# Re-timing the first transfers of a two-block transformer kernel and writing out the last turn of its branch loop

## The reference

```python
h = rmsnorm(x, g_pre_mix[l])
proj = h @ w_in[l]
(cb, cc, cv, q, k, v, qm, ga, gb, gc) = jnp.split(proj, IN_OFFSETS, axis=-1)
y_a = (cb * causal_dwconv(cc * cv, conv_mix_w[l])) @ w_conv_out[l]
...
y_b = jnp.transpose(o, (0, 2, 1, 3)).reshape(b_, s_, ATT_W) @ w_attn_out[l]
y_c = memory_attention(qm, rmsnorm(mem, g_mem[l]), w_mem_kv[l]) @ w_mem_out[l]
merged = (jax.nn.sigmoid(ga + bg[0]) * y_a + jax.nn.sigmoid(gb + bg[1]) * y_b
          + jax.nn.sigmoid(gc + bg[2]) * y_c)
x = x + rmsnorm(merged @ w_out[l], g_post_mix[l])
```

## Time and profile before

| | before |
|---|---|
| time, median of 3 runs | 1634.99 us |
| lowest and highest run | 1633.8 and 1635.36 us |
| time of the profiled execution | 1635.36 us |
| its span in the trace | 1633.6 us |
| PE busy | 1567.8 us, 96% of the span |
| DVE busy | 901.2 us, 55% |
| ACT busy | 627.0 us, 38% |

### The profile page before, as it was taken

One profiled execution on the slowest core, in us unless ns is written; L12 is line 12 of the kernel. 1 busy time (PEld: TensorE's weight loads), 2 busy tenths in 40 slices (PEclk: granted clock), 3 DMA queues, 4 the chain that ended last, 5 costly groups with the idle time before them and its releaser, 6 DMA issues.

```text
span 1633.6 us, 20708 instructions
## 1 busy us (share of the span) xinstructions
PE 1567.8 (96%) x7842; PEld 1311.6 (80%) x7842; DVE 901.2 (55%) x1441; ACT 627.0 (38%) x862; POOL 11.8 (1%) x16
## 2 busy tenths in 40 slices
PE   5999999999999899999999889998989999999999
PEld 5888787888877688888888767998878788888887
DVE  4443465544553877776532857978965444434322
ACT  5451434332233444444332535564463323232211
POOL 0000000000000000000000000000000000000000
PEclk9999999999999899999999999999999999999999
DMA  8312221222222122222322312202002222222222
GB/s 291 125 77 103 75 75 52 103 85 95 103 83 97 52 103 92 90 101 103 129 103 103 118 52 77 78 26 74 31 27 89 92 103 101 81 101 103 103 103 77
DMA packets 25705, 150.18 MB, mean 92 GB/s; under 512 B 2563, under 2 KB 4995, under 8 KB 9260
## 3 DMA queue, kind: packets, MB, share of 16 engines
q1 hardware_dynamic: 25644, 149.35, 26.1%
HBM read 147.21 MB, written 2.13 MB: 91 GB/s over the span
## 4 chain that ended last, share of the span: by engine, by line
PE 83%; DVE 9%; ACT 4%; issue 2%; SPq 1%; DMA 1%; DVEq 0%; ACTq 0%
PE bank L1676 25%; PE bank L1678 25%; PE bank L1677 25%; ACT w_hi L569 2%; PE bank L1790 2%; PE bank L2074 1%; PE bank L1770 1%; DVE w_lo L1033 1%; PE bank L2011 1%; DVE sel L1452 1%; DVE st L1451 1%; DMA raw<-weights 1%; PE bank L1779 1%; DVE w_lo L1041 1%; DVE mx L1163 0%
## 5 line engine op out<-in xcount | busy, mean ns | idle before, releaser
L1676 PE MATMUL bank<-h_hi,w_hi 128*128 128x512 f32 (+1 forms) x1200 | 475.7, 396 | 12.6 <-DVE h_lo L1106 9.9
L1033 DVE TENSOR_TENSOR w_lo<-raw,w_hi 128x2048 fp32r<-128x2048 f32 x118 | 270.3, 2291 | 369.3 <-ACT w_hi L569 368.9
L1678 PE MATMUL bank<-h_hi,w_lo 128*128 128x512 f32 (+1 forms) x1200 | 469.2, 391 | 0.0
L1677 PE MATMUL bank<-h_lo,w_hi 128*128 128x512 f32 (+1 forms) x1200 | 468.9, 391 | 0.0
L569 ACT ACTIVATE w_hi<-raw 128x2048 fp32r<-128x2048 f32 x128 | 244.5, 1910 | 345.7 <-PE bank L1678 342.5
L1676 PEld LDWEIGHTS bank<-h_hi,w_hi 128*128 128x128 f32 (+1 forms) x1200 | 225.5, 188 | 67.6 <-DVE h_lo L1106 9.4
L1678 PEld LDWEIGHTS bank<-h_hi,w_lo 128*128 128x128 f32 (+1 forms) x1200 | 225.5, 188 | 48.7
L1677 PEld LDWEIGHTS bank<-h_lo,w_hi 128*128 128x128 f32 (+1 forms) x1200 | 225.7, 188 | 47.3 <-issue 0.9
L1676 PE MATMUL bank<-a_hi,w_hi 128*128 128x512 f32 x352 | 136.9, 389 | 0.0
L1677 PE MATMUL bank<-a_lo,w_hi 128*128 128x512 f32 x352 | 136.9, 389 | 0.0
L1678 PE MATMUL bank<-a_hi,w_lo 128*128 128x512 f32 x352 | 136.9, 389 | 0.0
(11 more groups left out here) (283 smaller groups left out, 1913.1 us busy)
## 6 DMA issues: line engine op xcount, KB each, us to landing
raw<-weights SPq DMA_DIRECT2D x128, 1024.0 KB, 4.8
toep<-bias_scratch SPq DMA_DIRECT2D x8, 448.0 KB, 4.4
x<-xT SPq DMA_DIRECT2D x1, 2048.0 KB, 18.0
x_tok<-x_tok SPq DMA_DIRECT2D x1, 2048.0 KB, 15.9
outT<-x SPq DMA_DIRECT2D x8, 256.0 KB, 4.2
memT<-memT SPq DMA_DIRECT2D x2, 512.0 KB, 5.9
...
```

The lines of the kernel that those rows point to most:

```text
L1033: nc.vector.tensor_tensor(w_lo[m % 2][:, :], raw[m % 2][:, :], w_hi[m % 2][:, :].bitcast(F32), ALU.subtract).then_inc(lo_ready, 1)
L1676: nc.tensor.matmul(o, lh, rh, start=first, stop=False)
L1677: nc.tensor.matmul(o, lh, rl, start=False, stop=False)
L1678: return nc.tensor.matmul(o, ll, rh, start=False, stop=last)
```

## The change

It has two parts. At the start, `memT` and load 0 come in three pieces each (a quarter, a quarter, a half: `PIECES`), rounded and split piece by piece; `x` comes in two halves; load 2 is issued ahead of `x`, load 3 between the two halves and load 4 behind them, ahead of `x_tok`; `ident`, `onehot` and `rel_bias` come ahead of all of these; ACT and DVE round, split and scale in an order that follows this. In the branch loop the last of the three turns is written out as straight code on PE, ACT and DVE; in it ACT rounds the first four tiles of `merged` before it rounds the first load of `w_out`, and DVE makes the eight low parts between the last four merges instead of behind them.

```diff
@@ -463,26 +466,38 @@
                                  bass.AP(src.tensor, (2 * pair + j) * 1024, [[1, P], [1, 896]])
                                  ).then_inc(toep_in[pair % 2], 16)
 
-            def mem_half(c):
+            def mem_piece(c):
+                piece = slice(PIECES[c], PIECES[c + 1])
+                sp.dma_start(memT[:, piece, :], A["memT"].rearrange("(k p) t -> p k t", p=P)[:, piece, :]
+                             ).then_inc(mem_in[c], 16)
+
+            def raw_piece(c):
+                piece = slice(PIECES[c] * COLS, PIECES[c + 1] * COLS)
+                sp.dma_start(raw[0][:, piece], A["weights"][0, :, piece]).then_inc(raw_piece_in[c], 16)
+
+            def x_half(c):
                 half = slice(c * KT // 2, (c + 1) * KT // 2)
-                sp.dma_start(memT[:, half, :], A["memT"].rearrange("(k p) t -> p k t", p=P)[:, half, :]
-                             ).then_inc(mem_in[c], 16)
+                sp.dma_start(x[:, half, :], A["xT"].rearrange("(k p) t -> p k t", p=P)[:, half, :]).then_inc(x_in[c], 16)
 
             sp.dma_start(vec[:, :], A["vec"]).then_inc(vec_in, 16)
-            mem_half(0)
-            sp.dma_start(raw[0][:, 0:SLOT // 2], A["weights"][0, :, 0:SLOT // 2]).then_inc(raw_half, 16)
-            mem_half(1)
-            sp.dma_start(raw[0][:, SLOT // 2:SLOT], A["weights"][0, :, SLOT // 2:SLOT]).then_inc(raw_full[0], 16)
+            for c in range(3):
+                mem_piece(c)
+                raw_piece(c)
             load(1)
             sp.dma_start(mem_tok[:, :, :], A["mem_tok"].rearrange("(t p) d -> p t d", p=P)).then_inc(mem_tok_in, 16)
-            sp.dma_start(x[:, :, :], A["xT"].rearrange("(k p) t -> p k t", p=P)).then_inc(x_in, 16)
             sp.dma_start(ident[:, :], A["ident"]).then_inc(const_in, 16)
             sp.dma_start(onehot[0:NB + 1, :], A["onehot"]).then_inc(onehot_in, 16)
             sp.dma_start(relb[0:NB, :], A["rel_bias"]).then_inc(onehot_in, 16)
             sp.wait_ge(lo_ready, 1)
             load(2)
+            x_half(0)
+            sp.wait_ge(lo_ready, 2)
+            load(3)
+            x_half(1)
+            sp.wait_ge(lo_ready, 3)
+            load(4)
             sp.dma_start(x_tok[:, :, :], A["x_tok"].rearrange("(t p) d -> p t d", p=P)).then_inc(x_tok_in, 16)
-            stream(3, FIRST["v"] + 2)
+            stream(5, FIRST["v"] + 2)
 
             sp.wait_ge(bank_free[slot["bias", 1].bank], turn(("bias", 1)) + 1)
             sp.dma_start(A["bias_scratch"], bias_row[0:HEADS, :]).then_inc(bias_saved, 16)
@@ -655,18 +670,15 @@
             act.wait_ge(set_up, 1)
             nc.scalar.activation(st[:, 4, 15:16], ones[:, 0:1], ACT.Sqrt)
             act.wait_ge(vec_in, 16)
-            act.wait_ge(mem_in[0], 16)
-            for j in range(KT):
-                if j == KT // 2:
-                    act.wait_ge(mem_in[1], 16)
-                raised(mn_hi[:, j, :], memT[:, j, :], "g_mem", j)
-                if j == 1:
-                    act.wait_ge(raw_half, 16)
-                    nc.scalar.activation(w_hi[0][:, 0:SLOT // 2], raw[0][:, 0:SLOT // 2], ACT.Copy).then_inc(hi_half, 1)
-                if j == KT // 2:
-                    act.wait_ge(raw_full[0], 16)
-                    nc.scalar.activation(w_hi[0][:, SLOT // 2:SLOT], raw[0][:, SLOT // 2:SLOT], ACT.Copy
-                                         ).then_inc(hi_ready, 1)
+            for c in range(3):
+                act.wait_ge(mem_in[c], 16)
+                for j in range(PIECES[c], PIECES[c + 1]):
+                    raised(mn_hi[:, j, :], memT[:, j, :], "g_mem", j)
+                    if j == PIECES[c]:
+                        cut = slice(PIECES[c] * COLS, PIECES[c + 1] * COLS)
+                        act.wait_ge(raw_piece_in[c], 16)
+                        nc.scalar.activation(w_hi[0][:, cut], raw[0][:, cut], ACT.Copy
+                                             ).then_inc(hi_ready if c == 2 else hi_piece, 1)
 
             def token_squares(src, count, first):
 
@@ -678,18 +690,19 @@
             round_w(1)
             act.wait_ge(mem_tok_in, 16)
             token_squares(mem_tok, MT, 8)
-            act.wait_ge(x_in, 16)
+            root(MT, mean_ready, 1)
+            round_w(2)
             for j in range(KT):
+                if j % 4 == 0:
+                    act.wait_ge(x_in[j // 4], 16)
                 raised(h_hi[:, j, :], x[:, j, :], "g_pre_mix", j)
-                if j == 1:
-                    root(MT, mean_ready, 1)
-                    round_w(2)
-                if j == 5:
+                if j == 3:
+                    round_w(3)
+                if j == 4:
                     keep_rms("mem", rms_mem, M)
-                    round_w(3)
+            round_w(4)
             act.wait_ge(x_tok_in, 16)
             token_squares(x_tok, TT, 10)
-            round_w(4)
             act.wait_ge(rms_col, 1)
             for m in range(2):
                 for t in (2 * m, 2 * m + 1):
@@ -732,7 +745,13 @@
                 wait_own(("cb", t))
                 nc.scalar.activation(br_hi[:, t, :], cy[:, t, :], ACT.Copy).then_inc(rounded, 1)
 
-            with act.Fori(0, 3) as i:
+            def merged_hi(j):
+
+                act.wait_ge(merge_add, 4 + 16 + j + 1)
+                nc.scalar.activation(br_hi[:, j, :], merged[:, j, :], ACT.Copy).then_inc(rounded, 1)
+
+            def gates(i, last=False):
+
                 for half in range(2):
                     for m in range(3):
                         round_w(FIRST["branch"] + 3 * half + m + 1, i, 6)
@@ -743,10 +762,15 @@
                             nc.scalar.activation(gate[:, t, :], gate[:, t, :], ACT.Sigmoid,
                                                  bias=vec[:, bass.ds(8 * i + (VEC["b_gate"] + 4 * half + t), 1)]
                                                  ).then_inc(gated, 1)
-
-            for j in range(KT):
-                act.wait_ge(merge_add, 4 + 16 + j + 1)
-                nc.scalar.activation(br_hi[:, j, :], merged[:, j, :], ACT.Copy).then_inc(rounded, 1)
+                        if last and half and m == 1:
+                            for j in range(4):
+                                merged_hi(j)
+
+            with act.Fori(0, 2) as i:
+                gates(i)
+            gates(2, last=True)
+            for j in range(4, KT):
+                merged_hi(j)
             for m in range(4):
                 round_w(FIRST["w_out"] + m + 1)
                 for j in (2 * m, 2 * m + 1):
@@ -1204,26 +1228,29 @@
             dve.wait_ge(vec_in, 16)
             for j in range(KT):
                 low_gained(mn_lo[:, j, :], memT[:, j, :], "g_mem", mn_hi[:, j, :], j)
-                if j in (1, KT // 2):
-                    part_ = int(j > 1)
-                    cut = slice(part_ * SLOT // 2, (part_ + 1) * SLOT // 2)
-                    dve.wait_ge(hi_ready if part_ else hi_half, 1)
+                if j in PIECES:
+                    c = PIECES.index(j)
+                    cut = slice(PIECES[c] * COLS, PIECES[c + 1] * COLS)
+                    if c == 2:
+                        dve.wait_ge(hi_ready, 1)
+                    else:
+                        dve.wait_ge(hi_piece, c + 1)
                     nc.vector.tensor_tensor(w_lo[0][:, cut], raw[0][:, cut], w_hi[0][:, cut].bitcast(F32), ALU.subtract
-                                            ).then_inc(lo_ready if part_ else lo_half, 1)
+                                            ).then_inc(lo_ready if c == 2 else lo_piece, 1)
             split_w(1)
             dve.wait_ge(const_in, 16)
             token_norm(M, 8, 8)
+            split_w(2)
             for j in range(KT):
                 low_gained(h_lo[:, j, :], x[:, j, :], "g_pre_mix", h_hi[:, j, :], j)
-                if j == 1:
-                    split_w(2)
-                if j == 5:
+                if j == 3:
                     split_w(3)
-                    dve.wait_ge(bank_free[6], turn(("spread", "mem")) + 1)
-                    for t in (2, 3, 0, 1):
+                if j in (4, 6):
+                    for t in (2, 3) if j == 4 else (0, 1):
+                        dve.wait_ge(bank_free[6], turn(("spread", "mem")) + 1)
                         ready(("mem_k", t))
-                        frees(("mem_k", t), nc.vector.tensor_tensor(mk[:, t, :], B(("mem_k", t))[:, 0:M], rms_mem[:, :],
-                                                                    ALU.mult))
+                        frees(("mem_k", t), nc.vector.tensor_tensor(mk[:, t, :], B(("mem_k", t))[:, 0:M],
+                                                                    rms_mem[:, :], ALU.mult))
             split_w(4)
             token_norm(S, 10, 0)
             split_w(5)
@@ -1310,9 +1337,15 @@
                         dve.wait_ge(merge_add, 4 + 4 * half + t + 8 * i)
                         nc.vector.tensor_tensor(merged[:, 4 * half + t, :], merged[:, 4 * half + t, :],
```

(17 more changed lines are left out.)

17 lines of the change are left out of this document (11 added, 6 removed).

## The result

| | before | changed |
|---|---|---|
| time, median of 4 runs each on one chip | 1635.1 us | 1624.65 us |
| lowest and highest run | 1633.8 and 1635.36 us | 1623.29 and 1626.25 us |
| the profiled execution | 1635.36 us | 1623.29 us |

The ratio is 0.9934, with a 95% interval from 0.9922 to 0.9945: 10.5 us faster in the medians, 12.1 us between the two profiled executions. The forecast was 1622.9 us, with a range from 1620.3 to 1626.8.

A forecast was written before the change was run, and what follows sets the result against it. PE was taken as the bound, busy 1567.8 of 1633.6 us, so only its idle and low-clock stretches pay. 1635.36 - 11.7 (start) - 0.8 (join) = 1622.9 us, range 1620.3 to 1626.8.

The forecast's parts named there:

- The order of the transfers: Start: moving loads ahead of `x` and `x_tok` removes PE's waits; `qm` starts at 36.1, not 47.81, 11.7 us.
- The join: Last branch turn into first `w_out` tile: the 2.47 wait goes, split starts 2.2 later, gain 0.8; bounds +0.9 and -1.7.
- Load 2 ahead of `x`: Start: load 2 lands at 19.1, split by 23.4, before PE's 24.0; the 5.30 wait goes and PE stays at 2.4 GHz.
- Load 3 and `mk`: Start: load 3 lands at 24.3, `mem_k` banks free by 29.9, PE wants them at 30.3; 2.17 wait goes, 0.4 spare.
- A wait at load 3 for `mk`: Listed sign that the prediction is wrong: PE waiting at load 3 for `mk` or for the split.
- The pieces: Start: quarters of load 0 start PE near 7.5, but later landings stay the same; worth only 0.2 to 0.3 us.
- The rival of the longer low clock: Start: PE, fed in scattered bits, stays at 1.2 GHz, load 1 up to 4.7 us longer; 1625.5 to 1627.6, chance 0.12.
- `x_tok`: Start: issued behind load 4, lands at 34.7; load 5 split at 45.0, PE wants it at 48.0; hidden, 3 us spare.
- `ident`: Start: table ahead of `x` comes near 17, so the norm's root is out by 19.2, no longer waiting until 22.56.
- only as a bound: First `w_out` tile: -1.7 us, half of a 3.4 us stretch at clock 0.50 that isn't there, and no wait gap.
- Writing out the turn as such: Last branch turn: same PE matmuls, loop register instructions fall away; costed at nothing, hidden by matmuls without a gap.
- The sum: Whole kernel: profiled 1635.36 less 11.7 at the start and 0.8 at the join gives 1622.9 us.

The follow-up runs named there:

- run 1: Kernel before with only `memT` and load 0 in a quarter, a quarter and a half: 1635.14 us, ratio 1.0005.
- run 2: Changed kernel with `memT` and load 0 in two halves and the old branch loop, leaving the new order alone: 1623.87 us, ratio 0.9935.
- run 3: Kernel before with only the last branch turn written out and the low parts dealt in: 1635.31 us, ratio 1.0001.
- run 5: Like run 2, but only load 2 moved ahead; loads 3 and 4 behind all of `x` and `x_tok`: 1632.48 us, ratio 0.9982.
- Run 9: Run 7 with the first two `mk` tiles right behind load 3's split on DVE, ahead of the fifth low part: 1621.92 us, ratio 0.9926.
- run 11: Changed kernel, pieces included, with the old branch loop of three turns: 1623.4 us, ratio 0.9935.
- Run 6: Run 2 with `x_tok` one place further back, behind load 5: 1625.16 us, ratio 0.9941.
- Run 8: Run 2 with `ident`, `onehot` and `rel_bias` issued behind the first half of `x`: 1627.15 us, ratio 0.9946.
- run 10: The changed kernel itself measured again, in one group with runs 9 and 11: 1625.05 us, ratio 0.9943.
- run 4: Changed kernel with ACT's four copies of `merged` behind the rounding of `w_out`'s load instead of ahead: 1623.68 us, ratio 0.9939.
- run 7: Run 2's order, load 0 in two halves, with the written-out join of run 4: 1622.47 us, ratio 0.9929.

## Why the prediction was right

The order of the transfers was right in its mechanism and nearly in its size. The join was right in its steps and counted for a gain that the times don't show. That the profiled execution came within 0.4 us of the forecast is in part luck: of the changed kernel's ten executions only one was faster.

**Load 2 ahead of `x`: right.** It landed at 19.40 where I had 19.1 and was split at 23.64 where I had 23.4; PE wanted it 0.52 earlier, since in this execution the first landings came 0.9 sooner than I had them, and stayed at 2.4 GHz. Runs 1, 2 and 3 show that the gain is this order (with that of ACT and DVE behind it) and nothing else of the change; run 5 shows that the first step of it is worth little alone, because the queue then is late with load 3: the wait moves. Loads 3 and 4 were only ever moved together, so what load 4's place is worth alone is not shown.

**Load 3 and `mk`: the margin was too thin, as marked.** I had 0.4 to spare. Load 3 landed 1.4 later than I had it, and PE waited 0.87. A wait at load 3 for `mk` is one of the signs of being wrong that the prediction names, and this one came. Over the profiles with this order ACT began to round load 3 between 24.5 and 26.6, and the wait was between nothing and 1.40. It is most of the 0.8 that `qm` starts later than I had said. Run 9 takes one low part out of the way and has no wait; with one profile of it, that it never has one isn't shown.

**The pieces: worth nothing that the times show, where I had 0.2 to 0.3.** PE starts at 6.56 (I had 7.5), then waits for the end of load 0 and for load 1, whose landings are those of the same bytes. By my own numbers PE was 0.4 late at load 1 and not 0.2 (18.53 against 18.15); run 1 shows 0.3 of it won at the end of load 1 and lost again in the wait for load 2. Runs 2 and 11, without and with pieces and in different groups, stand at 1623.50 ± 0.61 and 1623.64 ± 0.44. The rival of the longer low clock, at 0.12, did not come in the changed kernel's two profiles, but it did in run 1's.

**`x_tok`: right.** It landed 1.1 later than I had it, and load 5 was split at 45.70 in place of 45.0. Run 6 confirms the chain of some 10 behind its landing, and that it begins to cost at a landing of 38.4.

**`ident`: right, and worth more than I thought.** The forecast only needed it to come near 17. Run 8 puts it, with the two other tables, behind the first half of `x` and loses 2 to 3 us of the 11.

**The join: the mechanism was right, the term was measured against the wrong thing.** The step that failed is "Before, the tile ended at 488.69. Gain 0.8." By the steps as I wrote them, PE ends the tile at 487.9, 19.6 behind the last gate; ACT takes it up 0.2 later, which makes 19.8, and the profiles of the changed kernel give 19.5 each time. But 488.69 held a low-clock stretch of 3.4 us behind the wait, which is not always there. The same old code needs 20.6 with it (the profiles before, 1, 5, 6 and 8) and 18.96 without (2 and 11). So the new code is worth a gain of 1.1 in the one case and a loss of 0.5 in the other. I had the stretch only as a bound. The times show no gain: by the means run 3 is 0.2 ± 0.5 slower than the kernel before, and run 10 is 1.3 ± 0.7 slower than run 11, with the start of `qm` in their profiles 1.2 apart for another reason. Whether the new join costs something or nothing on average is not settled. That the late split is what makes the new join no better is shown by run 4: without the delay the tile is done at 17.4.

**Writing out the turn as such: nothing, as costed.** The third turn takes 65.27 or 65.28 from gate to gate with the loop and without. From the start of `qm` to the last gate the kernels with the loop took 420.5 to 421.9 and those with the turn written out 420.3 to 421.9. The Trainium skill (Runtime: NRT & Kernel Launch, "Instruction fetch mechanics") calls a taken branch a possible stall in fetching; none is seen in these distances.

**The sum.** Between the two profiles the lead is 10.9 at the start of `qm`, 10.6 at the last gate (468.27 − 457.65; the stretch from 269.40 took some back), 11.7 behind the first `w_out` tile (488.89 − 477.15) and 12.1 at the end. The median run is 1.4 above the profiled one, which was the lowest of its four. The record has a mean granted clock for every run, and for the kernel before it goes with the time: over its 49 counted executions in the three groups each 0.001 more clock goes with 1.0 us less (correlation −0.83), from 1637.1 us on average at 0.984 to 1633.0 at 0.988. The 38 executions of the seven other kernels with the new order (runs 2, 4, 6 to 9 and 11) show the same, 1.0 us for 0.001 (−0.78). But the ten of the changed kernel don't (0.07): 1622.92 us was at 0.989 and 1626.25 at 0.990. As far as three digits of the clock can tell, it does not explain the 1.4, and what does is open. The forecast of 1622.9 was 0.4 below the profiled execution and 1.8 below the median. The sum had 0.8 too much at the start, and 0.8 for a join that is worth something only where the clock had fallen; without these two it gives 1624.5. The chances that the prediction lists for the single cases make 0.97 for faster, where it states 0.96.
